# Turning the FFN activations with VectorE blocks and a trip through HBM in place of TensorE transposes

## The reference, cut to what matters

```
def swiglu(x, w_gate, w_up, w_down):          # x (256, 1024), w_gate, w_up (1024, 2816), w_down (2816, 1024)
    return (jax.nn.silu(x @ w_gate) * (x @ w_up)) @ w_down
...
x = x + 0.5 * swiglu(rmsnorm(x, g), w_gate, w_up, w_down)                    # four times (layers 1)
x = layer_norm(DN_ALPHA * x + 0.5 * swiglu_ffn(x, w_in, w_out), g, b)        # four times (layers 2)
```

## Time and profile before

| what | value |
|---|---|
| median of 3 runs | 2496.46 us |
| profiled execution, its own time | 2496.44 us |
| its span | 2494.7 us |
| instructions | 31118 |
| granted TensorE clock, mean | 0.999 |
| TensorE (PE) busy | 2466.5 us, 99% |
| weight loads of TensorE (PEld) busy | 2105.8 us, 84% |
| VectorE (DVE) / ScalarE (ACT) / GpSimd (POOL) busy | 60% / 47% / 3% |
| HBM traffic | 458.30 MB, mean 184 GB/s |

### The profile page before, as it was taken

How to read it: one execution, slowest core, us unless ns; L and a number is a source line. 1 busy time by engine, 2 the same in 40 slices (tenths; PEclk the granted TensorE clock), 3 DMA queues, 4 the chain that set the end, 5 groups by cost and what they waited for, 6 DMA issues and landing times.

```text
span 2494.7 us, 31118 instructions
## 1 busy us (share of the span) xinstructions
PE 2466.5 (99%) x13042; PEld 2105.8 (84%) x13042; DVE 1505.7 (60%) x1533; ACT 1183.8 (47%) x1276; POOL 71.4 (3%) x116
## 2 busy tenths in 40 slices
PE   8999999999999999999999999999999999999998
PEld 6889998888889988888889878888888898788887
DVE  6545875555556775555557657655655567577554
ACT  5435544434436544444435564544344356644442
POOL 0000100000000100000000010000000000100000
PEclk9999999999999999999999999999999999999999
DMA  8555445455454446456545445454554544454542
GB/s 304 186 185 186 153 166 206 169 191 205 169 195 179 167 152 219 169 199 211 217 168 184 160 149 206 179 211 167 200 209 167 192 169 161 148 206 160 213 169 100
DMA packets 68195, 458.30 MB, mean 184 GB/s; under 512 B 7752, under 2 KB 9928, under 8 KB 15832
## 3 DMA queue, kind: packets, MB, share of 16 engines
q1 hardware_dynamic: 61488, 433.23, 47.7%
q0 software_dynamic: 4352, 20.45, 2.3%
q10 hardware_dynamic: 2216, 2.63, 0.5%
HBM read 453.65 MB, written 2.62 MB: 183 GB/s over the span
## 4 chain that ended last, share of the span: by engine, by line
PE 91%; DVE 4%; ACT 2%; issue 1%; DMA 1%; SPq 0%; POOL 0%; DVEq 0%; POOLq 0%; ACTq 0%
PE acc L594 24%; PE acc L596 24%; PE acc L595 24%; PE acc L562 4%; PE acc L563 4%; PE acc L564 4%; PE aux L666 2%; DVE w_lo L495 1%; PE aux L793 1%; ACT w_hi L487 1%; DMA raw<-in_w 1%; ACT tmp L1476 1%; PE stat L610 1%; PE bc L610 0%; PE aux L1164 0%
## 5 line engine op out<-in xcount | busy, mean ns | idle before, releaser
L495 DVE TENSOR_TENSOR w_lo<-raw,w_hi 128x2048 fp32r<-128x2048 f32 (+1 forms) x417 | 936.0, 2248 | 766.5 <-ACT w_hi L487 764.5
L487 ACT ACTIVATE w_hi<-raw 128x2048 fp32r<-128x2048 f32 (+1 forms) x417 | 782.7, 1880 | 635.6 <-PE acc L596 606.0
L594 PE MATMUL acc<-w_hi,x_hi 128*128 128x512 f32 (+1 forms) x1848 | 724.0, 392 | 3.8 <-DVE x_lo L1728 2.1
L596 PE MATMUL acc<-w_lo,x_hi 128*128 128x512 f32 (+1 forms) x1848 | 716.3, 388 | 0.0
L595 PE MATMUL acc<-w_hi,x_lo 128*128 128x512 f32 (+1 forms) x1848 | 715.7, 387 | 0.0
L594 PEld LDWEIGHTS acc<-w_hi,x_hi 128*128 128x128 f32 x1848 | 347.2, 188 | 77.0 <-issue 6.1
L596 PEld LDWEIGHTS acc<-w_lo,x_hi 128*128 128x128 f32 x1848 | 347.0, 188 | 72.0
L595 PEld LDWEIGHTS acc<-w_hi,x_lo 128*128 128x128 f32 x1848 | 347.3, 188 | 69.3 <-issue 1.0
L594 PE MATMUL acc<-w_hi,h_parts 128*128 128x512 f32 x704 | 275.4, 391 | 0.0
L596 PE MATMUL acc<-w_lo,h_parts 128*128 128x512 f32 x704 | 274.2, 389 | 0.0
L595 PE MATMUL acc<-w_hi,h_parts 128*128 128x512 f32 x704 | 273.9, 389 | 0.0
(11 more groups left out here) (394 smaller groups left out, 2188.2 us busy)
## 6 DMA issues: line engine op xcount, KB each, us to landing
raw<-in_w SPq DMA_DIRECT2D x399, 1024.0 KB, 4.8
raw<-in_w SPq DMA_DIRECT2D x18, 512.0 KB, 3.3
tmp<-in_norm_gb POOLq DMA_DIRECT2D x8, 1024.0 KB, 5.2
tmp<-in_norm_gb POOLq DMA_DIRECT2D x6, 512.0 KB, 3.9
tmp<-in_gate_rows POOLq DMA_DIRECT2D x12, 256.0 KB, 2.9
gates<-in_mixc POOLq DMA_DIRECT2D x2, 800.0 KB, 4.7
raw<-in_w SPq DMA_DIRECT2D x2, 800.0 KB, 4.4
skew<-tmp ACTq DMA_DIRECT2D x1, 1536.0 KB
```

Source lines behind the costliest of these rows:

```text
L487: nc.scalar.activation(w_hi[:, slot, 0:kind], raw[:, slot, 0:kind], ACT.Copy).then_inc(hi_done, 1)
L495: nc.vector.tensor_tensor(w_lo[:, slot, 0:kind], raw[:, slot, 0:kind], w_hi[:, slot, 0:kind].bitcast(F32), ALU.subtract).then_inc(lo_done, 1)
L594: nc.tensor.matmul(out, vh, wh, start=first and k == 0, stop=False)
L596: last = nc.tensor.matmul(out, vh, wl, start=False, stop=last_k and k == nk - 1)
```

## The change: what it does

In every FFN, TensorE no longer transposes HID. VectorE transposes each 32x32 block of HID in its place's own 32 partitions (`turn_squares`, two instructions for a block), giving `SQ` in `tmp[:, 24:28]`. GpSimd (`permute`) waits for both, stores SQ into an HBM scratch `squares` (one DMA, 512 KB, 256 KB for block 5; two scratch places in turn), waits until the store has landed, and loads it back with four DMAs, one for each group of 32 partitions, in runs of 1 KB, into one of two landing places `HF` in `tmp[:, 8:16]`. The order of the rows that comes out of it is not the plain one; the down weights are laid out to match on the host (`turned_rows`). `hid_high` and `hid_low` read HF through `landed` in place of PSUM, two blocks later in place of one; those of blocks 4 and 5 come behind the splits up to u = 27 and u = 28. The write of `skew` moves from step 2 of FFN 6 to its end (`bias_store`, still ScalarE's queue), and the read of BIAS moves to GpSimd's queue at the start of the first mixer 2, as two DMAs. The operand REL moves from `tmp` to `sm`.

```diff
+def turned_rows(w):
+    n = w.shape[0] // P
+    return rows_of(w.reshape(4, n, 32, -1).transpose(1, 0, 2, 3).reshape(w.shape))
...
+        SQ = flat(tmp[:, 24:28])
+        HF = [flat(tmp[:, 8 + 4 * i:12 + 4 * i]) for i in range(2)]
+        squares = nc.dram_tensor("squares", (2, P, 4 * S), F32, kind="Internal").ap()
...
-        REL = tmp[0:32, 12, 0:8]
+        REL = sm[0:32, 96:104]
...
+        def landed(i, tt):
+            w = tiles_of(i)
+            v = HF[i % 2][:, 0:w * S].rearrange("p (a t k j) -> p a t k j", a=4, t=2, j=32)
+            return v[:, :, tt].rearrange("p a k j -> p k a j")
...
@@ TensorE: x_turn, ffn @@
+                if N == 1 and tt == 0:
+                    pe.wait_ge(consts_loaded, 16 * N_CONSTS)
...
-                def turn(i):
-                    for tt in range(2):
-                        n = 12 * f + 2 * i + tt
-                        pe.wait_ge(hid_ready, n + 1)
...
-                        if n >= 2:
-                            pe.wait_ge(hid_parts, n - 1)
-                        for q in range(4 if i < 5 else 2):
-                            last = nc.tensor.transpose(aux[:, tt, q * P:(q + 1) * P], HID[:, tt, q * P:(q + 1) * P], ident[:, :])
-                        last.then_inc(hid_turned, 1)
...
-                    if j % 4 == 0 and j:
-                        turn(j // 4 - 1)
...
-                    if j == 0:
-                        turn(5)
@@ ScalarE: ffn @@
                 def hid_high(i):
+                    w = tiles_of(i)
+                    act.wait_ge(hid_landed, 64 * (6 * f + i + 1))
                     for tt in range(2):
-                        act.wait_ge(hid_turned, 12 * f + 2 * i + tt + 1)
...
+                        nc.scalar.activation(h_hi[:, 4 * i:4 * i + w, tt * P:(tt + 1) * P].rearrange("p k (a j) -> p k a j", j=32),
+                                             landed(i, tt), ACT.Copy).then_inc(hid_hi, 1)
...
-                    hid_high(i - 1)
+                    if i > 1:
+                        hid_high(i - 2)
                     silu(i, 0)
                     silu(i, 1)
...
-                ahead.to(c0 + 26)
+                ahead.to(c0 + 27)
+                hid_high(4)
+                ahead.to(c0 + 28)
                 hid_high(5)
                 if s == 6:
-                    act.wait_ge(e["skew_stored"], 16)
-                    act.dma_start(BIAS, skew[:, P:P + P * 383].rearrange("h (p w) -> p h w", w=383)[:, :, 0:S])\
-                        .then_inc(e["bias_loaded"], 16)
+                    bias_store()
...
@@ VectorE: ffn (times, turn_squares, hid_low) and mix2 @@
-                        dve.wait_ge(hid_turned, n - 1)
+                        dve.wait_ge(squares_ready, n - 1)
...
+                def turn_squares(i):
+                    w = tiles_of(i)
+                    n = 6 * f + i
+                    if n:
+                        dve.wait_ge(squares_stored[(n - 1) % 2], 16 * ((n - 1) // 2 + 1))
+                    for tt in range(2):
+                        V_.transpose(SQ[:, 0:w * S].rearrange("p (b t c) -> p b t c", b=4, t=2)[:, :, tt],
+                                     HID[:, tt, 0:w * P].rearrange("p (b c) -> p b c", b=4)).then_inc(squares_ready, 1)
...
-                        V_.tensor_tensor(h_lo[at], aux[:, tt, 0:w * P].rearrange("p (a b) -> p a b", b=P), h_hi[at].bitcast(F32),
-                                         ALU.subtract).then_inc(hid_parts, 1)
+                        to, hi = (v[:, 4 * i:4 * i + w, tt * P:(tt + 1) * P].rearrange("p k (a j) -> p k a j", j=32)
+                                  for v in (h_lo, h_hi))
+                        V_.tensor_tensor(to, landed(i, tt), hi.bitcast(F32), ALU.subtract).then_inc(hid_parts, 1)
...
-                    hid_low(i - 1)
+                    if i > 1:
+                        hid_low(i - 2)
...
                     times(i, 1)
+                    turn_squares(i)
...
-                ahead.to(c0 + 26)
+                ahead.to(c0 + 27)
+                hid_low(4)
+                ahead.to(c0 + 28)
                 hid_low(5)
...
-                dve.wait_ge(e["bias_loaded"], 16)
+                dve.wait_ge(e["bias_loaded"], 32)
@@ GpSimd: mix2, permute, and the loop over sub-layers @@
+                if l == 0:
+                    pool.wait_ge(e["skew_stored"], 16)
+                    for h in (0, 4):
+                        pool.dma_start(BIAS[:, h:h + 4], skew[h:h + 4, P:P + P * 383].rearrange("h (p w) -> p h w", w=383)[:, :, 0:S])\
+                            .then_inc(e["bias_loaded"], 16)
...
+            def permute(f, i):
+                n, w = 6 * f + i, tiles_of(i)
+                pool.wait_ge(squares_ready, 2 * (n + 1))
+                to = squares[n % 2, :, 0:w * S]
+                pool.dma_start(to, SQ[:, 0:w * S]).then_inc(squares_stored[n % 2], 16)
+                pool.wait_ge(squares_stored[n % 2], 16 * (n // 2 + 1))
+                if n >= 2:
+                    pool.wait_ge(hid_parts, 2 * (n - 1))
+                for b in range(4):
+                    src = to[:, b * w * 64:(b + 1) * w * 64].rearrange("(a r) c -> r a c", a=4)
+                    pool.dma_start(HF[i % 2][32 * b:32 * b + 32, 0:w * S].rearrange("r (a c) -> r a c", a=4), src).then_inc(hid_landed, 16)
...
+                    for i in range(6):
+                        permute(subs[:s].count("ffn"), i)
```

More of the change, by code:

```diff
@@ L83, in ffn_weights @@
         for j in range(5):
-            out[WIDE].append(rows_of(w[512 * j:512 * j + 512]))
-        out[HALF].append(rows_of(w[2560:]))
+            out[WIDE].append(turned_rows(w[512 * j:512 * j + 512]))
+        out[HALF].append(turned_rows(w[2560:]))
 def pack(i):
@@ L344, in program @@
         first_loaded, first_hi, first_lo = sem("first_loaded"), sem("first_hi"), sem("first_lo")
-        silu_ready, hid_ready, hid_turned, hid_hi, hid_parts = (
-            sem(n) for n in ("silu_ready", "hid_ready", "hid_turned", "hid_hi", "hid_parts"))
+        silu_ready, hid_ready, squares_ready, hid_hi, hid_parts = (
+            sem(n) for n in ("silu_ready", "hid_ready", "squares_ready", "hid_hi", "hid_parts"))
+        squares_stored = [sem(f"squares_stored{i}") for i in range(2)]
+        hid_landed = sem("hid_landed")
         v_chain, a_chain, g_chain = (sem(n) for n in ("v_chain", "a_chain", "g_chain"))
@@ L376, in program, with flat @@
         e.update({n: sem(n) for n in names3})
+        def flat(ap):
+            return ap.rearrange("p a b -> p (a b)")
         GB = tmp[:, 28:36].rearrange("p a b -> p (a b)")
@@ L443, in program, with tiles_of @@
         JUNK1 = QT[:, 0]
-        def flat(ap):
-            return ap.rearrange("p a b -> p (a b)")
         def ps(tile):
             return acc[:, tile % RING, :]
+        def tiles_of(i):
+            return 4 if i < 5 else 2
         def split_at(ap, li):
@@ L1259, in hid_high @@
                 def hid_high(i):
+                    w = tiles_of(i)
+                    act.wait_ge(hid_landed, 64 * (6 * f + i + 1))
                     for tt in range(2):
-                        act.wait_ge(hid_turned, 12 * f + 2 * i + tt + 1)
-                        w = 4 if i < 5 else 2
-                        nc.scalar.activation(h_hi[:, 4 * i:4 * i + w, tt * P:(tt + 1) * P],
-                                             aux[:, tt, 0:w * P].rearrange("p (a b) -> p a b", b=P), ACT.Copy).then_inc(hid_hi, 1)
+                        nc.scalar.activation(h_hi[:, 4 * i:4 * i + w, tt * P:(tt + 1) * P].rearrange("p k (a j) -> p k a j", j=32),
+                                             landed(i, tt), ACT.Copy).then_inc(hid_hi, 1)
                 if s == 0:
@@ L1407, in bias_copy, with bias_store @@
                 nc.scalar.activation(STAGE, stat[0:8, 0:384], ACT.Copy).then_inc(e["rel_copied"], 1)
+            def bias_store():
                 act.wait_ge(e["rel_copied"], 1)
@@ L1822, in ffn @@
                 times(0, 1)
+                turn_squares(0)
                 ahead.to(c0 + 7)
```

4 lines of the change are left out of this document (removed).

## The result

The changed kernel takes 2457.01 us (median of four runs, 2456.84 to 2457.09). The kernel before takes 2496.47 (2496.27 to 2496.50). The ratio is 0.9842, with a 95% interval of 0.983 to 0.9854: 39.5 us less. The forecast was 2457.0. The profiled execution took 2456.84 us, with a span of 2455.0.

A forecast was written before the change was run, and what follows sets the result against it. TensorE's own instruction stream was taken to bound the kernel: 2496.44 us less 39.4 for the removed transposes, plus 0 for everything added or moved, gives 2457.0 us. Its own range was 2455 to 2460, and 2453 to 2466 for 8 in 10.

The forecast's parts named there:

- What bounds: Whole kernel: TensorE's own instruction stream sets the end, busy 2466.5 of 2494.7 us, at full clock.
- the removed slots: TensorE in the eight FFNs: 352 transposes gone, worth 39.4 us by cadence, 38.3 by the chain of waits.
- VectorE's part: FFNs: two added transposes per block, 0.68 us each for 128x512, 7.8 us per FFN, all beside TensorE.
- rival (c): VectorE becomes the bound if a transpose costs over 5.0 us; at 6 us, 84 us more, time 2541; chance 0.01.
- `hid_high` and `hid_low` from SBUF: FFNs: reading SBUF in place of PSUM leaves their times unchanged, 0.54 and 0.68 us; worth 0.
- The round trip: GpSimd and DMA, each FFN block: transposes, store and loads take 10.7 to 15.5 us, 13 taken; spare 12 to 14.
- The date of block 5: FFN's end: the trip must be done 25.0 us after `times`, before TensorE opens u = 27.
- The date of blocks 0 to 4: FFNs: `hid_high` comes 27.5 us after `times`; if late, ScalarE waits, with two `silu` and the next splits behind it.
- Rival (a): Trip misses its date: TensorE waits at u = 27 for the excess over 25.0 us, eight times; chance 0.04.
- Rival (b): FFN's end and next norm: late splits cost 2 to 3 us per FFN, 20 us, time 2477; chance 0.07.
- rival (d): TensorE in the FFNs: the transposes were free, their slots are filled otherwise, time 2496; chance 0.02.
- Rival (e): GpSimd's five issues each wait out a VectorE split, trip 27.0 us at worst, time 2473; chance 0.01.

The follow-up runs named there:

- idle transposes: Changed kernel with 352 transposes of the identity, read by nobody, put back on TensorE in their old places: 2497.24 us.
- Nine pairs: Changed kernel with each pair of VectorE block transposes made nine times, only the last counting: 2558.08 us.
- the four added stores: Changed kernel with four more 256 KB stores into a second scratch, each waited for, before block 5's store in each FFN: 2506.14 us.
- four pairs: Changed kernel with each pair of VectorE block transposes made four times, only the last counting: 2455.91 us.
- the kernel with three chunks: Changed kernel with `hid_high` of block i-1 in step i, behind `silu` and the split of u = 4i+6, `hid_low` behind `turn_squares`(i): 2457.08 us.

## Why the prediction came out right, step by step

- *What bounds* and *the removed slots*. Shown. 39.4 us from cadences, 39.5 measured. The mechanism is right; that the forecast meets the median to the tenth is luck, since 1 us between programs is not explained and the two readings of the rows were 1.1 us apart. The idle transposes bring back 40.2. Eight at 0.107 and 0.054 for the place are 0.91 us a group, near the cadence's 0.89; the lower end of 38.3, from the chain alone, left out the cost of the place.
- *VectorE's part*. 0.68 us was taken from `hid_low`; the group after says 691 ns, and 0.65 us apart in the timeline. The load that decides was put at over 5.0 us for a transpose. Nine pairs, 12.0 us, are as much as two transposes of 6.0, for which rival (c) gave a block of 23.9 us (23.7 measured) and 84 us; the waits were 76 and the cost 101. The Trainium skill ("VectorE: DVE Perf Modes", The three transpose paths) gives 311 ns for a 128x128 bf16 block; four of them would be 1.24 us, an estimate for a 128x512 instruction. The trace has 0.69, so it disagrees for float32.
- *`hid_high` and `hid_low` from SBUF*. One `hid_high` took 613 ns against 585 before, one `hid_low` 684 against 682: nothing.
- *The round trip*. 13 was taken of 10.7 to 15.5. The median of 11.5 us lies inside, but the upper end was too low already in the changed kernel: 16.6 us for block 0 of the second FFN, 18.3 at most. The range was a sum of median landings, while single loads take up to 9.9 us to land and stores up to 6.0. The spare of 12 to 14 us covered this, so the time did not feel it.
- *The date of block 5*, 25.0 us. Shown by the four added stores: 3.0 over it in the second FFN, 3.3 us of wait on average.
- *The date of blocks 0 to 4*, called the softer one. Here the reasoning fell short, though the number did not feel it. The prediction named the `silu` and splits that stand behind a late `hid_high`, but made no price of them; they close a loop from block to block, and one block nearer costs 125 us. The distance of two blocks is what keeps this away: the trip has 28.3 us there and takes 18.3 at most. With 17.5 us it still costs nothing, with 6.6 it does.
- *Rival (a)'s price*, eight times the excess. Too low, since it had a term for the wait and none for the clock: 112 us of waits came to 141. Its point of no gain lies below 29.9 us: with a trip of 28.0 in the second FFN the kernel was already slower than before.
- *Rival (b)*, small waits of the new way, and *rival (d)*, transposes that were free. The kernel without any turning is only 1.1 us faster than the changed one, which leaves (b) at most that; the idle transposes, at 40.2 us, exclude (d).
- *Rival (e)*, GpSimd's issues held up by VectorE. Issues stay at 0.56 us, and the loads' landing doesn't go with the splits beside them. The starvation of which the Trainium skill warns ("SBUF — State Buffer", the box on the DVE blocks DMA trap) is not to be seen beside splits. Beside block transposes no run tests it: GpSimd issues only when they are done, with one pair as with four or nine. In the second FFN of the kernel with four the loads have also landed before the next pairs begin (block 1's at 431.7, the next pairs at 432.3). So the longer landings with four pairs (7.0 us against 4.5) have another cause. In block 1 of the second FFN two weight loads are issued there within 1.5 us of the four loads, at 418.1 and 420.3 around 419.6; that this is the cause is argued, not shown.
- *The bias move*, 0. Shown, with the write's landing at 1258.1 us, well within its 97 us of cover.
- *Weight loads*, 0. Their median landing is unchanged at 4.8 us at a DMA share of 0.69.

What stays open: the 1 us between programs with and without the turning, 13 us of the kernel with nine pairs and 5 of the one with the blocks taken up one later, and whether distance or order does it in the kernel with three chunks.

## What to carry to other kernels

Where one engine has nothing in front of it but its own stream, price what is taken off it by the cadence of the work around it (here 0.89 us a group), not by busy time. Work put on other engines cost nothing here, as long as each handover met its date and no engine's load passed the period; so work out the date of each, and also walk every handover round until it comes back to itself: if a late one stands ahead of the work that the next one needs, in the same engine's order, the round must fit into one period, or must be stretched over two. Price a missed date higher than the wait, as the clock falls with it, and sum a trip from the worst landings beside other traffic rather than from medians.

## What was not expected of the hardware

- The same four loads land in 2.8 us (3.4 at most) from SP's queue, ahead of the next weight load, and in 4.5 (9.9) from GpSimd's, beside them.
- The wait for a 256 KB store was 2.0 to 2.2 us or 5.3 to 5.4.
- The write of `skew`, 1.5 MB, was issued at 1220.0 and had landed at 1258.1 in the changed kernel, 38 us.
- After 12.9 idle us TensorE ran at 1.2 GHz for 3.6 us (matmuls 0.43 us apart from 542.3 to 545.9).
